# Ring slots freed by their last product, and weight units split ahead of the normalised tiles, in a 14-step block kernel on one core

## The reference: what is computed

```python
for i in range(DEPTH):                                   # 4
    mod = (silu(c) @ ada_w[i] + ada_b[i])                # shift, scale, gate of the three parts
    h = adaln(x, norm_g[i, 0], shift[:, 0], scale[:, 0])
    x = x + 0.5 * gate[:, 0] * swiglu(h, ffn_w_in[i, 0], ffn_w_out[i, 0])
    h = adaln(x, norm_g[i, 1], shift[:, 1], scale[:, 1])
    y = rwkv7 | mamba2 | windowed attention | rwkv7      # by layer
    x = x + gate[:, 1] * y
    h = adaln(x, norm_g[i, 2], shift[:, 2], scale[:, 2])
    x = x + 0.5 * gate[:, 2] * swiglu(h, ffn_w_in[i, 1], ffn_w_out[i, 1])
```

## Time and profile before

| what | value |
|---|---|
| median of three runs | 3226.04 us (3223.27 to 3228.61) |
| the profiled execution, its own time | 3215.61 us |
| its span, first to last instruction | 3213.9 us |
| mean granted TensorE clock | 0.969 |
| PE busy | 3077.8 us, 96% of the span |
| DVE / ACT / POOL busy | 2373.2 / 1399.8 / 97.0 us |
| moved by DMA | 609.47 MB, mean 190 GB/s |

### The profile page before, as it was taken

The page is one execution under the profiler, slowest core; times in us unless marked ns, Lnnn a source line. Parts: engine busy times, 40 slices in busy tenths (PEclk is TensorE's granted clock), DMA queues, the critical chain, the costliest instruction groups (busy, mean ns, idle before and its releaser), DMA issues.

```text
span 3213.9 us, 49803 instructions
## 1 busy us (share of the span) xinstructions
PE 3077.8 (96%) x19866; PEld 2706.3 (84%) x19866; DVE 2373.2 (74%) x3501; ACT 1399.8 (44%) x2222; POOL 97.0 (3%) x187
## 2 busy tenths in 40 slices
PE   7999989999999999999999999999989999999998
PEld 6887788888889888888886888887788888989887
DVE  6978863788886876888867888877752876765685
ACT  4534121454545663545444554533111544465453
POOL 0000000000000000000000000000000000000000
PEclk9999997999999999999999999999998999999899
DMA  8774422567675335675764666662200553444453
GB/s 344 256 274 157 183 68 69 214 234 283 239 280 207 146 119 219 228 290 205 261 238 162 240 261 231 240 236 99 112 1 26 198 190 138 158 159 149 157 186 131
DMA packets 69670, 609.47 MB, mean 190 GB/s; under 512 B 7728, under 2 KB 7888, under 8 KB 31824
## 3 DMA queue, kind: packets, MB, share of 16 engines
q1 hardware_dynamic: 42768, 459.41, 38.6%
q0 software_dynamic: 26352, 144.88, 12.1%
q10 hardware_dynamic: 336, 2.13, 0.2%
HBM read 604.30 MB, written 2.10 MB: 189 GB/s over the span
## 4 chain that ended last, share of the span: by engine, by line
PE 84%; DVE 11%; ACT 2%; issue 1%; DMA 1%; SPq 0%; DVEq 0%; POOLq 0%; ACTq 0%
PE psum L323 26%; PE psum L926 23%; PE psum L930 12%; PE psum L947 10%; PE psum L954 6%; PE psum L321 4%; PE psum L951 1%; PE psum L1697 1%; DVE ada_sum L505 1%; DMA weights<-in_weights 1%; DVE arena L812 1%; PE psum L1646 1%; DVE arena L2303 1%; DVE wkv_base L2069 1%; DVE small L2068 1%
## 5 line engine op out<-in xcount | busy, mean ns | idle before, releaser
L877 ACT ACTIVATE unit_high<-weights 128x1024 fp32r<-128x1024 f32 x594 | 628.7, 1060 | 710.4 <-PE psum L930 391.6
L883 DVE TENSOR_TENSOR unit_low<-weights,unit_high 128x1024 fp32r<-128x1024 f32 x594 | 725.8, 1223 | 201.1 <-ACT unit_high L877 200.5
L926 PE MATMUL psum<-h_part,unit_high 128*128 128x512 f32 x3168 | 822.4, 396 | 21.6 <-DVE h_part L799 14.1
L926 PEld LDWEIGHTS psum<-h_part,unit_high 128*128 128x128 f32 x3168 | 577.1, 191 | 131.1 <-issue 16.6
L930 PEld LDWEIGHTS psum<-h_part,unit_low 128*128 128x128 f32 x3168 | 445.8, 192 | 29.5
L930 PE MATMUL psum<-h_part,unit_low 128*128 128x256 f32 x3168 | 467.5, 284 | 0.0
L323 PE MATMUL psum<-in_part,w_part 128*128 128x256 f32 x2784 | 359.6, 289 | 8.0 <-issue 4.7
L323 PEld LDWEIGHTS psum<-in_part,w_part 128*128 128x128 f32 x2784 | 346.5, 195 | 24.2 <-issue 11.0
L947 PE MATMUL psum<-hidden,unit_high 128*128 128x512 f32 x1386 | 353.9, 396 | 0.0
L1053 DVE TENSOR_REDUCE arena<-psum 128x256 f32<-128x512 f32 x396 | 272.8, 689 | 61.1 <-PE psum L930 49.6
L323 PE MATMUL psum<-arena 64*128 64x128 f32 (+7 forms) x2304 | 272.7, 293 | 32.1 <-DVE arena L2154 9.1
(11 more groups left out here) (310 smaller groups left out, 2783.0 us busy)
## 6 DMA issues: line engine op xcount, KB each, us to landing
weights<-in_weights SPq DMA_DIRECT2D x290, 1536.0 KB, 6.5
ada_in<-in_ada_w POOLq DMA_DIRECT2D x182, 768.0 KB, 5.9
consts<-in_consts POOLq DMA_DIRECT2D x1, 1700.0 KB, 16.3
x<-in_x SPq DMA_DIRECT2D x1, 1024.0 KB, 8.8
v_first<-arena ACTq DMA_DIRECT2D x1, 1024.0 KB, 6.0
arena<-v_first ACTq DMA_DIRECT2D x1, 1024.0 KB, 4.7
weights<-in_weights SPq DMA_DIRECT2D x1, 512.0 KB, 5.6
out<-x SPq DMA_DIRECT2D x1, 512.0 KB, 2.6
```

The lines of the kernel that those rows point to most:

```text
L877: k.nc.scalar.activation(k.unit_part[0][:, n % UNIT_RING], w, ACT.Copy).then_inc(k.sem["unit_high"], 1)
L883: k.nc.vector.tensor_tensor(k.unit_part[1][:, n % UNIT_RING], w, k.unit_part[0][:, n % UNIT_RING].bitcast(FP32), ALU.subtract).then_inc(k. ...
L926: mm(k.psum[:, 2 * (j % 2) + half, :].rearrange("p (i t) -> p i t", i=2), lhsT=part(2 * j + half, 0, t), rhs=k.h_parts[:, :, t], start=t = ...
```

## The change

It has four parts.

1. In `first_mod_products` the last product of a slot gives the slot back itself, where before the first product on the next slot did. `spread_rstd` of norm 0 moves from behind all of these products to a place ahead of the last round (r == 3), which is where slot 4 begins. The last, partly filled slot 5 is now given back by `turn_mod_rows`, with a drain ahead of it.
2. At norm 0 ACT writes the high parts of the units 0 and 1 ahead of all tiles, and not behind the third; DVE writes unit 0's low part between `mod_rows` and `mod_columns`, and unit 1's behind the first tile's low part. The low part of a tile is written one tile behind the scaling (`lag` = 1), not two.
3. Behind RWKV (n = 2 and n = 11) ACT writes two high parts ahead of the norm's root and the third behind it, where all three stood behind the root; DVE writes unit 0's low part ahead of the reciprocal and unit 1's behind it, where both stood behind it.
4. In all nine FFNs PE waits at the first tile for each part of a unit where it is first used.

```diff
@@ first_mod_products
+        if r == 3:
+            spread_rstd(k, pe, pr, 0)
         for t in range(OPENING_SUMMED if r < 2 else 0, KT):
             for g in range(4):
-                pr.mm(k.psum[32 * g:32 * g + 32, 3, 256:384], k.c_pick[:, t, 23 - r:55 - r], pr.take(),
+                w, used = pr.take(), pr.block % BLOCKS == 0
+                if used:
+                    pr.freed = True
+                pr.mm(k.psum[32 * g:32 * g + 32, 3, 256:384], k.c_pick[:, t, 23 - r:55 - r], w,
                       (r, t) == (0, OPENING_SUMMED), (r, t) == (3, KT - 1),
-                      k.sem["mod_rows"] if (r, t, g) == (3, KT - 1, 3) else None)
+                      k.sem["mod_rows"] if (r, t, g) == (3, KT - 1, 3) else k.sem["weights_used"] if used else None)
     pr.align()
-    spread_rstd(k, pe, pr, 0)
     turn_mod_rows(k, pe, pr, 0)
@@ norm_act
+    after_rwkv = 0 < n < NORMS and SUBS[n - 1] == "rwkv"
+    for u in range(2 if after_rwkv else 0):
+        unit_high(k, act, ffn, u)
     norm_root(k, act, n)
-    if 0 < n < NORMS and SUBS[n - 1] == "rwkv":
-        for u in range(3):
-            unit_high(k, act, ffn, u)
+    if after_rwkv:
+        unit_high(k, act, ffn, 2)
     if ffn is not None:
         for t in range(KT):
-            if n == 0 and t == 3:
+            if n == 0 and t == 0:
                 for u in range(2):
                     unit_high(k, act, ffn, u)
@@ norm_vector
-    src = k.x if src is None else src
+    src, lag = k.x if src is None else src, 1 if n == 0 else 2
     if n < NORMS:
         dve.wait_ge(k.sem["mod_ready"], n + 1)
+    after_rwkv = 0 < n < NORMS and SUBS[n - 1] == "rwkv"
+    if after_rwkv:
+        unit_low(k, dve, ffn, 0)
     if n:
         norm_reciprocal(k, dve, own, n)
-    if 0 < n < NORMS and SUBS[n - 1] == "rwkv":
-        for u in range(2):
-            unit_low(k, dve, ffn, u)
+    if after_rwkv:
+        unit_low(k, dve, ffn, 1)
@@ norm_vector, the tiles
-        if t >= 2:
-            low(t - 2)
-        if t == 3 and n == 0:
-            for u in range(2):
-                unit_low(k, dve, ffn, u)
+        if t >= lag:
+            low(t - lag)
+        if t == lag and n == 0:
+            unit_low(k, dve, ffn, 1)
@@ ffn_products
-    for w in range(2):
-        unit_wait(k, pe, i, w)
     for t in range(KT):
         pe.wait_ge(sem["h_ready"], k.h_at + t + 1)
         for half in range(2):
+            if t == 0:
+                pe.wait_ge(sem["unit_high"], FFN_UNITS * i + half + 1)
             up_high(0, half, t)
+            if t == 0:
+                unit_wait(k, pe, i, half)
             up_low(0, half, t)
@@ build, the vector engine
-            mod_vector(k, dve, own, 0)
+            mod_rows(k, dve, 0)
+            unit_low(k, dve, 0, 0)
+            mod_columns(k, dve, own, 0)
```

More of the change, by code:

```diff
@@ L822, in norm_vector @@
             between(t)
-    for t in (KT - 2, KT - 1):
+    for t in range(KT - lag, KT):
         low(t)
-    if n == 0 or n < NORMS and SUBS[n - 1] == "rwkv":
+    if n == 0 or after_rwkv:
         unit_low(k, dve, ffn, 2)
```

## The result

| | before | changed |
|---|---|---|
| median of 20 executions each | 3221.14 us (3214.78 to 3228.61) | 3214.95 us (3206.47 to 3223.23) |
| profiled execution: own time, span | 3215.61, 3213.9 us | 3206.47, 3204.7 us |
| mean granted clock | 0.969 | 0.970 |

The ratio is 0.9983, with an interval of 0.9975 to 0.9991: 5.5 us less (2.9 to 8.1), which is inside the 0.2% that I took as the same. The median of 3226.04 in the table ahead was that of three executions. With 17 more the kernel before stands at 3221.14, and in the experiments, on four chips, its medians of 29 to 35 executions go from 3215.86 to 3221.28.

What follows compares the result with a forecast made beforehand. PE bounds the kernel (84% of the chain of waits), so only its standing time can be won. Opening 1.1 and norms 1.1 and 1.2 sum to 3.4 us: 3226.0 - 3.4 = 3222.6 us, range 3217 to 3229.

Steps and rivals of the forecast that it cites:

- 1.1 + 1.1 + 1.2 = 3.4: Microseconds gained in the opening and at the two norms behind RWKV, summed; the forecast's case had chance 0.59.
- Slot 6 issued at 24.2, DMA at full from 26 on: Opening: SP issues slot 6 3.4 us earlier than 27.63, and the DMA share stays near 1 from 26 to 30.
- T at 31.3: Opening: T, when ACT can begin unit 0's high part, comes 2.5 us earlier than 33.80; bounds 30.7 and 31.9.
- if the last engine to be free decides: Opening: slot 6's transfer follows only at 27.8, so ACT can begin unit 0's high part at 31.9; lead 0.5 us.
- The chain to tile 1 at T + 6.35: Opening: PE reaches tile 1 6.35 us after ACT can begin unit 0, at 37.65 against 38.77, a 1.1 us lead.
- the second rival: Opening gives nothing: slot 6 arrives as late, the longer chain costs 1.4 us; sum 0.9 us, 3225 us; chance 0.14.
- I leave slot 4 at 27.04: Opening: slot 6's earlier issue doesn't delay slot 4, since an engine consumes a ring's descriptors in order.
- Behind RWKV, scaling 3.75 us behind the squares: First norm behind RWKV: DVE scales at 587.3 instead of 588.43, 1.1 us earlier; 1.2 us at n = 11.
- The clock's rise follows PE's start: Opening and first RWKV: the clock rises 5.4 us behind PE's start, so the lead stays whole at 3.4 us.
- the first rival: Clock rises much earlier in the opening and behind RWKV: gain 6.1 us, 3220 us, at most 8.8; chance 0.20.
- The split waits of PE at nothing: Six FFNs not behind RWKV or in the opening gain nothing; at most 0.14 us each, 1.3 at nine places.
- The root held by the high parts: Rival behind RWKV: slot missing, root waits behind the first high part; 9.8 us slower, 3236 us; chance 0.05.

Runs made afterwards that it cites:

- open_only: Kernel before with the changed opening and PE's split waits, the norms behind RWKV as before: 3218.32 us, 0.9996 of before.
- one_high: Changed kernel with one high part ahead of the root behind RWKV, not two: 3220.17 us, 0.9997 of before.
- three_highs: Changed kernel with all three high parts ahead of the root behind RWKV, not two: 3217.28 us, 1.0001 of before.
- rwkv_only: Kernel before with only the new order behind RWKV, opening and PE's waits as before: 3217.19 us, 0.9987 of before.
- release_only: Kernel before with only this changed: a slot's last product in the opening gives it back: 3217.21 us, 1.0001 of before.
- before_d: Kernel before, unchanged, run again on the fourth chip: 3221.34 us, 1.0003 of before.
- before_c: Kernel before, unchanged, run again on the fourth chip: 3214.94 us, 0.9987 of before.
- columns_first: Changed kernel with DVE's modulation columns and two scaled tiles ahead of unit 0's low part: 3213.66 us, 0.9991 of before; repeated on another chip 3214.84 us, 0.9974.
- order_only: Kernel before with the opening's new order and split waits, slots given back and norms behind RWKV as before: 3221.48 us, 1.0017 of before.
- after_again: Changed kernel, unchanged, profiled a second time: 3214.19 us, 0.9979 of before.

## Why the prediction was wrong, step by step

**What failed is the level.** The step reads "The median of the runs shown is 10.4 us above that execution, so I forecast 3226.0 - 3.4 = 3222.6 us". It took a median of three for the kernel's time. Over 20 executions that median is 3221.14, 4.9 us lower, and that is 4.9 of the 7.65 us by which the forecast missed. The range has the same fault: "the runs shown spread by 2.7 us to either side of their median" is three executions, while 20 spread from 3214.78 to 3228.61. With the right level, 3221.1 - 3.4 = 3217.7 us, and 3214.95 would have been inside a range as wide. With medians of before from 3215.86 to 3221.28 on four chips, even many executions on one chip leave a level of some microseconds open. The other 2.8 us are the gain (6.2 us between the medians, 5.5 by the ratio, whose interval of 2.9 to 8.1 holds 3.4). The call that it is the same within 0.2% held. The chances given to the four cases add up to 0.98; the text has no word on the other 0.02.

**The sum came near by luck.** 1.1 + 1.1 + 1.2 = 3.4 was forecast. The five profiles of the changed kernel have, on average, 0.06 behind the opening, 2.07 around the first norm (575 to 600) and 1.00 around the second (2480 to 2520): 3.1 us. The three unchanged copies of before average -0.15, 0.17 and -0.09 there. The 1.0 us that is missing in the opening is made up at the first norm, mostly by a clock that rose earlier than forecast.

- *Slot 6 issued at 24.2, DMA at full from 26 on.* Right: 24.48, and 23.98 to 25.17 in the others; the share 1.15 and 0.94.
- *T at 31.3.* Too early. ACT got the slot at 31.86, 32.54, 32.77, 32.96 and 32.34, on average 32.5; in the four profiles of before at 33.80, 34.51, 33.73 and 33.97, on average 34.0. The gain is 1.5 us and not 2.5. (One of these, 34.51, isn't the slot's: it had landed at 34.19, and ACT was held by the tiles.) The landing took 7.4 to 8.5 us after the issue, and the bound "if the last engine to be free decides" (31.9) was no bound but the best case. The sixteen increments of the slot's semaphore show how: the first comes at 30.26 to 30.79 in the five profiles, near the 30.7 of the lower bound and 2.7 us earlier than before on average, but the last at 31.84 to 32.94, 1.4 us earlier. Before, first and last were 0.6 to 0.9 us apart, now 1.6 to 2.4. The 0.5 us "for the landing" in that bound has no row and no run shows it by itself.
- *The chain to tile 1 at T + 6.35.* Right: 38.23 - 31.86 = 6.37, in all five. Before it was T + 4.97, so 1.5 us earlier at 1.4 us longer leaves 0.1: tile 1 is reached at 38.86 on average over the five profiles and at 38.97 over the four of before. The lead at 60 says so too: over the eight profiles that have the changed opening (the five, open_only, one_high with 0.63, three_highs with -0.42) it averages 0.02, over the five that have before's (rwkv_only with them) 0.03. So the opening is worth nothing and the norms make the gain, which is the outcome of the second rival ("The opening gives nothing"), by half of its mechanism: the slot did come earlier, and the longer chain took it back.
- *"I leave slot 4 at 27.04."* Right in this profile (26.97), not in others: 27.64, 27.82 and 27.47 in copies, 28.01 in release_only. In the six profiles with the late release it is at 26.86 to 27.12. The Trainium skill, "DMA: Bandwidth & Descriptors", section "Queues, rings and completion order", has an engine take a ring's descriptors in order, and I had put that against a delay. The runs show slot 4 0.4 to 1.0 us later in five of the eleven profiles with the early release. It is slot 4's last increments that are late (27.97 for the sixteenth in release_only, where fifteen had come by 26.39, against 27.00 and 26.91 before). What delays it was not measured, so the page isn't shown wrong, but as a forecast of the arrival it didn't do. It costs nothing in the changed kernel, since the rows are copied by 31.8 and aren't wanted before 33.
- *Behind RWKV, scaling 3.75 us behind the squares.* 3.66. PE starts 1.29 to 1.30 us earlier in all five at the first norm, where 1.1 was forecast, and 1.15 to 1.32 at the second, where it was 1.2. The root 0.5 later: 0.44. That is against before's first profile, in which the clock was full while PE summed the squares. Where it fell in the sum, the root of before had to wait, and PE started 7.09 to 7.33 us behind the squares and not 6.67 to 6.72 (before_d at both norms, before_c at the second), while the changed kernel's two high parts cover a sum that ends by 1.80: PE after 5.38 in nine of ten places, 5.54 in the tenth. This cover was in no term of the forecast.
- *The clock's rise follows PE's start.* The rise does, but the 5.4 us of both rows are one of several values. Behind the first RWKV the rise came 3.3 us after PE's start in four of the five profiles of the changed kernel, which is the gain of 0.94 to 1.02 in the table's third column of figures, and 5.6 in the fifth, which has none. In the changed kernel:

```profile
584.00:588.00 4.00, 4.00 (x18) 3.45 (x17) 4.00 (x12) 2.88 (x6) 0.00 (x0) 0.66 0.00 0
```

The clock is low until 586.7 there, PE having started at 583.36. I had named a rise within 4 us as what would prove the forecast wrong, and here the first rival happened, at one place of three and for 1 us of its 3.6. Behind the second RWKV the rise came after 3.2, 5.1, 5.9, 6.0 and 6.1 us, and took some of the 1.3 back. The Trainium skill, "TensorE: Matmul & The Clock Gate", section "What's actually happening", has this transition wander from run to run, by half a microsecond to either side. That it wanders the traces bear out; its size here is larger, with 2.9 to 6.8 us over all places and kernels. rwkv_only and columns_first have the same order of work behind RWKV and 5.5 us, and before_d, a kernel before, has 3.9, so the early rise is not shown to be the change's.
- *The split waits of PE at nothing.* Nearly: open_only and order_only, which have them without the new order behind RWKV, start PE 6.58 us behind the squares at the first norm, where before and release_only have 6.67, and rwkv_only without them starts at 5.47 where the changed kernel has 5.38. So 0.09 of the 1.30 us is theirs. Elsewhere open_only shows no gain beside the clock's steps (-7.59 at 600, -7.48 at the end).
- *The root held by the high parts.* It never waited for the slot in any of the profiles; three_highs shows what it costs when it stands too far back.

**What stays open.** The gain by time averages 4.9 us over the four comparisons (6.0, 6.3, 4.9, 2.4), the places show 3.1. By the errors of 1.1 to 1.4 us each, a mean of the four has one of 0.6, and 1.8 would be beyond chance. But by the same errors before_c, which is the kernel before, would be faster than itself. So either the errors are too small and nothing is left to explain, or the changed kernel meets a little less low clock elsewhere (rival B, in small). The fourth chip, with a clock 0.0003 higher only, speaks for the first; I couldn't settle it.

**The best version**, by the opening, is columns_first. Its tile 1 is reached 4.9 us behind the slot's arrival in both profiles against 6.37 (36.78 and 37.70), its leads at 60 are the two largest of all (2.27, 1.09; the next is 0.81), and it measured 0.9991 and 0.9974 of before. By time alone it can't be told from the changed kernel (3214.84 against 3217.83 on one chip, where executions of one kernel spread by over 10 us).

## What to carry to other kernels

When a gain of 0.1% is at stake, the time of a few executions is not the measure. Take the start of a same-numbered product at both ends of the place that was edited, in several profiles of each kernel: 1.30 us repeated to 0.01 at the first norm, while the medians of identical programs moved by 6.4. Take several profiles of the kernel before too: one of its copies was 0.41 us off at that place, by the clock. Forecast the level from many executions, not from a median of three.

Giving a buffer back earlier moves the issue by more than the arrival: 3.15 us against 1.94 in the profile shown, since the last of a transfer's sixteen increments decides. Count what the queue still holds, and don't let the consumer's chain grow by what the arrival gains: here a low part in front of small work that could have been done in the wait ate 1.4 of 1.5 us, and putting the small work back in front regained it.

## What the runs showed of the hardware

- The same program gets its low-clock stretches at different places from one execution to the next: in the same 20 us the clock was 1.00 or 0.66, and the lead over one execution fell by 6.3 us and rose by 7.9 within 155 us (after_again).
- 1536 KB issued while earlier slots were in flight landed 7.4 to 8.5 us after the issue in the five profiles of the changed kernel, its first and last increment 1.6 to 2.4 us apart; issued at 27.4 to 27.9, after the DMA share had fallen to 0.11 (first profile), it took 6.2 to 6.3 in the four of before, the increments 0.6 to 0.9 us apart. Fifteen of sixteen could be there almost 1 us before the last (30.92 and 31.84).
- PE's clock rose 2.9 to 6.8 us after PE's start; in the same place of the same program 3.3 in one execution and 5.6 in another.
